# A two-block transformer kernel on one core: rounding before the sigmoid in the gate tiles, one earlier release of PSUM, and a projection moved from the second expert to the third

## The reference, cut to what matters

```
hid = silu(einsum(xs, w_gate)) * einsum(xs, w_up)          # first block, per expert
ye  = einsum(hid, w_down) * gate
...
h = rms_norm(x, norm_mix_g)                                # second block
(q, k, v, z_a, gk_low, cb, cc, xc, z_c, g_a, g_c) = split(h @ w_in)
y_a = (rms_norm(o, gla_norm_g) * silu(z_a)) @ w_branch_a
y_c = ((cb * causal_dwconv(cc * xc)) * silu(z_c)) @ w_branch_c
merged = sigmoid(g_a + b_ga) * y_a + sigmoid(g_c + b_gc) * y_c
x = x + merged @ w_out
ple_gate = sigmoid(rms_norm(x, norm_ple_g) @ w_ple_gate)
x = x + ple_gate * (p @ w_ple_proj)
return rms_norm(x, norm_final_g)
```

## Time and profile before

| what | value |
|---|---|
| median of three runs | 1756.01 us (1751.14, 1756.01, 1756.23) |
| the profiled execution | 1751.84 us, span 1750.0 us |
| PE busy | 1292.9 us, 74% |
| DVE busy | 556.6 us, 32% |
| ACT busy | 421.8 us, 24% |
| DMA moved | 520.96 MB, mean 298 GB/s |
| chain that ended last | DMA 47%, PE 27%, DVE 11%, ACT 7% |

### The profile page before, as it was taken

One profiled execution on the slowest core, in us unless ns is written; L12 is line 12 of the kernel. 1 busy time (PEld: TensorE's weight loads), 2 busy tenths in 40 slices (PEclk: granted clock), 3 DMA queues, 4 the chain that ended last, 5 costly groups with the idle time before them and its releaser, 6 DMA issues.

```text
span 1750.0 us, 18932 instructions
## 1 busy us (share of the span) xinstructions
PE 1292.9 (74%) x8202; PEld 765.0 (44%) x8202; DVE 556.6 (32%) x774; ACT 421.8 (24%) x545; POOL 170.9 (10%) x69
## 2 busy tenths in 40 slices
PE   2688789778357676666666676767676899978896
PEld 0458789763122121112111111211111799977895
DVE  2656685530101110111011011101101596554564
ACT  1444466422000000000000000000000553445543
POOL 0425555710000000000000000000000000000000
PEclk8899889989678877888878778887877999989997
DMA  9484234774979999999999999999999545533450
GB/s 352 153 304 134 74 98 134 271 290 191 419 301 416 420 417 416 417 420 416 416 418 418 415 416 420 416 416 417 419 416 409 181 146 168 169 121 121 161 177 24
DMA packets 165523, 520.96 MB, mean 298 GB/s; under 512 B 10288, under 2 KB 94256, under 8 KB 129600
## 3 DMA queue, kind: packets, MB, share of 16 engines
q1 hardware_dynamic: 163072, 517.49, 75.9%
q10 hardware_dynamic: 2368, 2.26, 0.4%
HBM read 518.66 MB, written 1.05 MB: 297 GB/s over the span
## 4 chain that ended last, share of the span: by engine, by line
DMA 47%; PE 27%; DVE 11%; ACT 7%; issue 3%; SPq 3%; POOL 0%; ACTq 0%; DVEq 0%
PE B L1459 16%; DMA xslot<-in_wu 12%; DMA xslot<-in_wg 12%; DMA xslot<-in_wd 8%; DMA wslot<-in_wg 5%; DMA wslot<-in_wu 4%; PE B L1713 3%; SPq L418 3%; PE B L1758 2%; DMA wslot<-in_w_in 2%; ACT whj L450 2%; DVE wslot_r L1112 2%; DMA ctx<-in_ctx 2%; DMA wslot<-in_wd 2%; DMA wslot<-in_wpp 1%
## 5 line engine op out<-in xcount | busy, mean ns | idle before, releaser
L1713 PE MATMUL B<-xslot,xs 128*32 128x512 f32 x1496 | 240.2, 737 | 127.6 <-DMA xslot<-in_wu 79.3
L1758 PE MATMUL B<-xslot,hidT 128*32 128x512 f32 x784 | 158.8, 729 | 65.3 <-DMA xslot<-in_wd 57.0
L1713 PEld LDWEIGHTS B<-xslot,xs 128*32 128x32 f32 x1496 | 36.3, 117 | 299.6 <-DMA xslot<-in_wu 158.9
L1459 PE MATMUL B<-hnh,whj 128*128 128x256 f32 x496 | 145.5, 293 | 21.2 <-DVE wslot_r L1112 21.2
L1374 POOL TENSOR_TENSOR wslot_r<-wslot,whi 128x2048 fp32r<-128x2048 f32 x30 | 138.9, 4638 | 197.7 <-ACT whi L450 197.7
L1112 DVE TENSOR_TENSOR wslot_r<-wslot,whj 128x2048 fp32r<-128x2048 f32 x52 | 118.9, 2288 | 87.2 <-ACT whj L450 87.2
L1459 PE MATMUL B<-hn_r,whj 128*128 128x256 f32 x496 | 143.4, 289 | 0.0
L1459 PE MATMUL B<-hnh,wslot_r 128*128 128x256 f32 x496 | 142.4, 287 | 0.0
L1713 PE MATMUL B<-wslot,xs 128*32 128x512 f32 x552 | 95.3, 783 | 43.5 <-DMA wslot<-in_wu 28.0
L450 ACT ACTIVATE whj<-wslot 128x2048 fp32r<-128x2048 f32 x52 | 98.9, 1907 | 61.6 <-PE B L1459 55.4
L1758 PEld LDWEIGHTS B<-xslot,hidT 128*32 128x32 f32 x784 | 32.0, 120 | 182.0 <-DMA xslot<-in_wd 130.4
(11 more groups left out here) (415 smaller groups left out, 2095.0 us busy)
## 6 DMA issues: line engine op xcount, KB each, us to landing
xslot<-in_wd SPq DMA_DIRECT2D x98, 1024.0 KB, 20.0
xslot<-in_wg SPq DMA_DIRECT2D x94, 1024.0 KB, 21.4
xslot<-in_wu SPq DMA_DIRECT2D x93, 1024.0 KB, 26.8
wslot<-in_w_in SPq DMA_DIRECT2D x58, 1024.0 KB, 5.2
wslot<-in_wu SPq DMA_DIRECT2D x35, 1024.0 KB, 27.1
wslot<-in_wg SPq DMA_DIRECT2D x34, 1024.0 KB, 21.7
wslot<-in_wd SPq DMA_DIRECT2D x30, 1024.0 KB, 21.3
aslot<-in_ada_w SPq DMA_DIRECT2D x19, 1024.0 KB, 6.6
```

The lines of the kernel that those rows point to most:

```text
L1459: mm = e.matmul(ps, l, r, start=k == 0 and j == 0, stop=k == kn - 1 and j == 2)
L1713: mm = e.matmul(B[b][32 * j:32 * j + 32, :], XS[:, k, 32 * x:32 * x + 32], slots[r][:, 512 * j:512 * j + 512], start=k == 0, stop=k == 7)
L1758: mm = e.matmul(B[3 + db][32 * j:32 * j + 32, :], hidT[:, 128 * c + 32 * j:128 * c + 32 * j + 32], v2(slots[r])[:, j % 2, 512 * db:512 * d ...
```

## The change

Four pieces. On PE and ScalarE the product `pp` moves from x = 1 to x = 2. On ScalarE `hi(n+3)` comes first in each of the 16 gate tiles, then the sigmoid, then the rounding of the tile before. On VectorE the clamp of tile i comes first, then the two products of tile i-1 (the first frees its PSUM bank), then `lo(n+3)`, and last the rest of tile i-1. In the `wo2` tiles the squares for the norm and the addition of each pair of them are made tile by tile on both engines, in place of four squares and one wide addition behind `wpg` 0's preparation; `lo` of `wpg` 2 and 3 come behind the last pair. The number of arithmetic instructions on PE and ScalarE stays, VectorE has three more.

```diff
--- before.py
+++ after.py
@@ scalar @@
-                if x == 1:
+                if x == 2:
                     for c in range(4):
                         e.wait_ge(*p_misc.at("pp", c))
                         e.activation(pp0[:, 512 * c:512 * c + 512], B[5 + c % 2], ACT.Copy).then_inc(*a_left("pp", c))
...
             for name in ("zc", "zo"):
                 for hh in range(4):
+                    hi(NO[name, hh] + 3)
+                    sigmoid(tp2[hh % 2], name, hh)
                     if (name, hh) != ("zc", 0):
                         rounded(*(("zc", 3) if hh == 0 else (name, hh - 1)))
-                    sigmoid(tp2[hh % 2], name, hh)
-                    hi(NO[name, hh] + 3)
             for name, buf in (("ga", GA), ("gc", GC)):
                 for hh in range(4):
+                    hi(NO[name, hh] + 3)
+                    sigmoid(pair(buf, hh), name, hh)
                     if (name, hh) == ("ga", 0):
                         rounded("zo", 3)
-                    sigmoid(pair(buf, hh), name, hh)
-                    hi(NO[name, hh] + 3)
...
                     e.activation(HNh[:, k, :], XX[:, k, :], ACT.Identity, scale=vc_("nple", k)).then_inc(*a_h("h3", k))
-            if NO["wpg", 0] + 3 < NT:
-                hi(NO["wpg", 0] + 3)
-            for q in range(4):
-                if q == 0:
+                if c == 0:
                     e.wait_ge(*v_left.at("a2", 3))
-                e.activation(sqa[:, 2 * q:2 * q + 2, :], XX[:, 2 * q:2 * q + 2, :], ACT.Square).then_inc(*a_step("ple", q))
+                e.activation(sqa[:, 2 * c:2 * c + 2, :], XX[:, 2 * c:2 * c + 2, :], ACT.Square).then_inc(*a_step("ple", c))
+            hi(NO["wpg", 0] + 3)
@@ vector @@
+            def silu2(name, hh):
+                x, dst = pair(into_of[name][0], hh), tp2[hh % 2]
+                e.wait_ge(*a_sig.at(name, hh))
+                e.tensor_tensor(dst, dst, B_of[name, hh], ALU.mult).then_inc(*v_left(name, hh))
+                e.wait_ge(*v_left.now())
+                if name == "zo":
+                    e.wait_ge(*v_step.at("o2", hh, 1))
+                e.tensor_tensor(x, x, dst, ALU.mult).then_inc(*v_mid(name, hh))
+
+            def rest_of(name, hh):
+                x, x_h, x_l = (pair(y, hh) for y in into_of[name])
+                e.wait_ge(*a_h.at(name, hh))
+                e.tensor_tensor(x_l, x, x_h.bitcast(F32), ALU.subtract).then_inc(*v_h(name, hh))
+
+            gates2 = [(name, hh) for name in ("zc", "zo") for hh in range(4)]
+            for i, (name, hh) in enumerate(gates2):
+                if i == 0:
                     e.wait_ge(*v_step.at("att", 0))
-                clamp(dst, ps, name, hh)
+                elif i >= 2:
+                    e.wait_ge(*v_mid.at(*gates2[i - 2]))
+                clamp(tp2[hh % 2], B_of[name, hh], name, hh)
+                if i:
+                    silu2(*gates2[i - 1])
                 lo(NO[name, hh] + 3)
+                if i:
+                    rest_of(*gates2[i - 1])
...
+                    if (name, hh) == ("ga", 0):
+                        silu2("zo", 3)
                     lo(NO[name, hh] + 3)
+                    if (name, hh) == ("ga", 0):
+                        rest_of("zo", 3)
...
-                if NO["wo2", c] + 3 < NT:
+                e.wait_ge(*a_step.at("ple", c))
+                e.tensor_tensor(sqa[:, 2 * c, :], sqa[:, 2 * c, :], sqa[:, 2 * c + 1, :], ALU.add).then_inc(*v_mid("ple", c))
+                if c < 3:
                     lo(NO["wo2", c] + 3)
-            e.wait_ge(*a_step.at("ple", 3))
-            e.tensor_tensor(sqa[:, 0:4, :], sqa[:, 0:4, :], sqa[:, 4:8, :], ALU.add).then_inc(*v_mid("ple"))
-            if NO["wpg", 0] + 3 < NT:
-                lo(NO["wpg", 0] + 3)
+            lo(NO["wpg", 0] + 2)
+            lo(NO["wpg", 0] + 3)
@@ tensor @@
-                if x == 1:
+                if x == 2:
                     e.wait_ge(*l_pp.at())
                     e.wait_ge(*l_pT.at())
...
-            e.wait_ge(*v_mid.at("ple"))
+            e.wait_ge(*v_mid.at("ple", 3))
             for k in range(4):
-                mm = e.matmul(B[4][:, 0:256], ones, sqa[:, k, :], start=k == 0, stop=k == 3)
+                mm = e.matmul(B[4][:, 0:256], ones, sqa[:, 2 * k, :], start=k == 0, stop=k == 3)
```

More of the change, by code:

```diff
@@ L750, in scalar @@
             for c in range(4):
-                if NO["wo2", c] + 3 < NT:
-                    hi(NO["wo2", c] + 3)
+                hi(NO["wo2", c] + 3)
                 for k in (2 * c, 2 * c + 1):
@@ L1281, in vector @@
                     v_step.name("att", hh)
-            def silu2(name, hh, into):
-                dst, x, ps = tp2[hh % 2], pair(into, hh), B_of[name, hh]
-                if name == "zc" and hh == 0:
-                    e.wait_ge(*v_step.at("att", 0))
-                clamp(dst, ps, name, hh)
-                lo(NO[name, hh] + 3)
[L1290 to L1305, removed]
+            into_of = dict(zc=(C2, C2h, C2l), zo=(o2, o2h, o2l))
+            def silu2(name, hh):
[6 more added lines that the diff above has]
+                e.tensor_tensor(x, x, dst, ALU.mult).then_inc(*v_mid(name, hh))
@@ L1306, in vector @@
             for name, buf, off in (("ga", GA, 0), ("gc", GC, 8)):
                 for hh in range(4):
-                    flush()
                     e.wait_ge(*p_proj.at(name, hh))
```

## The result

The changed kernel took 1699.20 us as the median of four runs (1697.71 to 1701.38), the kernel before 1755.95 (four runs). The ratio is 0.9684, with a 95% interval of 0.9664 to 0.9704: faster by 3.2%, or 57 us. The profiled execution took 1701.38 us, with a span of 1699.6.

What follows compares the result with a forecast made beforehand. Transfers were taken to bound the experts, a circle through both vector engines the gate tiles. Gains of 36.3 + 7.1 + 11.1 = 54.5 us took 1751.84 to 1697.3; the middle level gave 1699.4, range 1692 to 1713.

Steps and rivals of the forecast that it cites:

- two levels: Whole program: runs shown lie at 1751.1 or 1756; the forecast took the middle, 1699.4, above 1697.3.
- The gate tiles: 17 tiles from the end of `zc` 0: VectorE's cycle 5.35 us, PE sets the pace at 5.66; gain 36.3 us.
- The lead of 7.0 us: Gate tiles: `lo(i+3)` is done at 4.3 us, PE needs it at 11.3, so longer cycles first use up 7.0 us.
- The tail: Norm sums and last gates around `wpg`: sums without a wait, last gate at 1729 not 1736.06; gain 7.1 us.
- The product: Moved to the third expert, it closes the transfer hole between 499 and 511 us; gain 11.1 us.
- rival 1: Third expert: SP, held at tile 65, lets the queue run dry; 11.1 us come back, 1708.4 or 1712.6; chance 0.07.
- Rival 2: Gate tiles: handing over between engines keeps a cycle of 7.0 us; PE loses 14.6 us, time 1712; chance 0.05.
- Rival 3: Tiles behind `zc` 0: PE's clock falls under denser work, up to 1883 us, slower than before; chance 0.03.
- No change: Gate tiles: `lo` is late because of loads, not the order; time stays 1752 to 1756; chance 0.03.

Runs made afterwards that it cites:

- e0: The changed kernel run once more with nothing altered: 1698.13 us, 0.9665 of the kernel before.
- e2: Kernel before with only the new ScalarE and VectorE order in the 16 gate tiles: 1718.23 us, 0.9791 of before.
- e7: Changed kernel with four more clamps on VectorE ahead of the products of each silu tile: 1708.19 us, 0.9724 of the kernel before.
- e8: Changed kernel with two more clamps on VectorE ahead of the products of each silu tile: 1696.47 us, 0.9672 of the kernel before.
- e9: Changed kernel with VectorE making the previous silu tile's products behind `lo`, not ahead of it: 1697.49 us, 0.9675 of the kernel before.
- e4: Kernel before with only the `hi` call moved first on ScalarE in the 16 gate tiles: 1719.12 us, 0.9781 of before.

## Why the prediction was right

**The time.** 1699.4 was predicted and 1699.2 measured. That it fits to 0.2 us is luck. The sum against the profiled execution was 54.5 us, and the three stretches show 53.8 in the changed kernel's trace, 56.1 in e0's and 55.1 with the mean over all traces for the experts. The profiled execution of the changed kernel took 1701.4, not 1697.3; 3.4 us of that are its later start at the experts, and 1.3 that its stretch from there to `zc` 0 gained 9.8 us and not 11.1; the other two terms give 0.7 back. I read two levels into the three times shown, and took the middle between them; the kernel before, run ten more times, fell anywhere between 1750.7 and 1759.9. It is a spread, and the middle was right for another reason than mine.

**The gate tiles: 36.3 predicted, 36.7 measured** (e2 alone the same). The bookkeeping on both engines held. VectorE's list is even shorter than the 5.35 us I had. It takes 4.73 by itself (e7, e8), since I let it wait for the rounding, from 4.3 to 4.65, and took its instructions longer than they are from start to start (clamp to product 0.61 us, not 0.68). The other 0.4 us are small change: PE's 17 tiles took 5.653 us each and not 5.66 (0.1), and the tiles behind 1647.46 were not quite at full pace before, six in 34.19 us, 5.70 each (0.3). That the earlier release of PSUM adds nothing is shown by e9. What I had not seen is that all of the new order but one call adds nothing either (e4): my working showed that the new lists allow 5.66 us, and I did not ask which single move would.

**The lead of 7.0 us** held up: none was needed in the changed kernel, and e7 and e8 show it as a reserve, once what stands ahead of `lo` is taken off it.

**The tail: 7.1 predicted, 7.3 to 7.4 measured.** The last clamp chain starts 18.6 us behind `wpg` 0 (1685.62 less 1666.98) where it was 26.05. The gates on VectorE start 4.60, 4.93 and 4.95 us apart, from the late 1671.14 on, and reach the last one just when PE has made its last tile: the chain runs through VectorE from `wpg` 0 to the end. The measured 7.3 to 7.4 lie at the upper bound of 7.3 or a tenth above it. The forecast of 1729 for the last gate, 19.0 us behind `wpg` 0, was 0.4 us too late, because the first distance is 4.60 us and not about 5.0.

**The product: 11.1 predicted, 11.0 measured** as the mean over eleven traces; in single traces, against the one of the kernel before, it is 9.7 to 12.3, so that a fit to 0.1 us is luck. SP was held, as rival 1 said, for 11.2 us, and the transfers went on at 421 GB/s. PE made the product in 7.07 us, from 523.99 on, at a granted clock of 1.00, and not in 9.44, where the clock was 0.75 (from 499.04 to 508.48). The row of 28.12 us which rival 1 took as the trace's word for the rule holds SP's wait for a slot of 14.4 us, between one issue that took 8.23 us and seven more. The wait is as the rule says, and half as long as the row.

**Rival 2** (a chain in the gates) would have needed a cycle above 5.65 us plus the lead's share; VectorE's list takes 4.73. **Rival 3** (the clock falls under denser work): the granted clock is 1.00 in all 90 us of the gates, and 26 tiles in a row ran at 5.65 us each without a break. **No change** is out by e2.

## What to carry to other kernels

Write down, for each of two engines that hand work to each other, what each step waits for, and look for a circle that doesn't contain the engine you want busy. One call in the wrong place (the preparation of later weights behind a wait for the present result) cost 37 us of 1750, and moving that one call got all of it back. In a stretch bound by transfers, look for the windows in which nothing is transferred and for the one issue that holds the rest of the queue: a hole costs about its length (here 12 us, where PE stood still for 42.8), and a held issue costs nothing as long as enough is out ahead of it (here nine tiles, 22.6 us of transfers, against a hold of 11.2).

## What the runs showed of the hardware

Executions of one kernel spread over 9 us, and by the traces most of that lies ahead of the second block (start 416.0 to 420.8 us, the experts another 3 us), while the 28 tiles behind `zc` 0, up to `wpg` 0, took 158.28 us in nine kernels, each time to the hundredth. In this stretch a microsecond can be placed in one trace; the intervals of the medians are 6 to 11 us wide.

A wait costs PE more than its length, since the granted clock is lower behind it: the eight records of sums took 3.67 us behind a wait of 5.5 us, at a granted clock of 0.53 from 1715.39 to 1719.06, and 1.89 us without a wait, at 1.00 from 1666.7 to 1668.7.
